# Reading the moving operand of the dense matmuls backwards, and writing PSUM backwards with it

## The chip, the cores and the metric

The kernel runs on one core of a Trainium2 chip. The metric is the device time of the whole kernel in microseconds (us), the median of several executions; lower is better. TensorE (PE in the rows) multiplies a stationary operand of up to 128 by 128 elements, loaded by a weight load (PEld), with a moving operand that is streamed through it column by column; the result goes to PSUM, eight banks of 512 float32 columns on each of 128 partitions. The other engines are VectorE (DVE), ScalarE (ACT), GpSimd (POOL) and SyncE (SP, which here issues the weight transfers).

## The reference, cut to what matters

One inference step of a two-layer decoder trunk for 256 prompt tokens and 8 sample tokens: a diagonal state-space layer, then an attention layer with compressed, selected and window branches. Nearly all of its arithmetic is dense products with float32 weights:

```python
D_MODEL, SEQ, DEC_BATCH, D_FF, PLE_DIM = 2048, 256, 8, 5632, 256

def swiglu(h, wg, wu, wd):
    return (jax.nn.silu(h @ wg) * (h @ wu)) @ wd

def compress_rows(rows, w1, b1, w2):        # paged K and V rows of 8 sequences of 2048
    ...
    w1p = w1.reshape(CMP_PARTS, CMP_STRIDE, HEAD_DIM, CMP_HIDDEN)
    h = b1
    for j in range(CMP_PARTS):
        h = h + jnp.einsum('bnsgd,sdh->bngh', units[:, j:j + n_cmp], w1p[j])
    return jax.nn.gelu(h) @ w2

# per layer: mixer, then x + swiglu(...), then
#   x = x + gate * (p[i] @ w['ple_w_proj'][i])   with gate from a 2048 x 2048 product
# between the layers: kv = rmsnorm(h) @ kv_w;  in the mixers: g @ w_glu, hn @ w_q, o @ w_o
```

## The kernel before

**Layout.** All activations stand transposed: channels on the partitions, the T = 264 tokens (256 prompt, 8 sample) as columns. A weight tile of 128 by 128 is the stationary operand and a [128, 264] slice of the activations the moving one.

**Precision.** A float32 product is made from three matmuls of the reduced type fp32r. A weight unit of 1024 columns is copied from `w_raw` to `w_head` by ScalarE (`split_head`, L377, which rounds), and VectorE takes the rest, `w_rest` = `w_raw` - `w_head` (`split_rest`, L381). The activations are split in the same way (`act_head` and `act_rest`, `hid_head` and `hid_rest`, `ple_head` and `ple_rest`). The product is then head by head, head by rest and rest by head, all three added into the same PSUM columns (L396, L397, L398).

**Dense groups.** `group_matmuls` goes through the units of a group. In each unit there are UK = 2 slices of the contraction, and for each slice four output tiles in four neighbouring PSUM banks, three matmuls each: 24 matmuls a unit. `phase_pe` calls it for the phases gate/up, down, per-layer embedding, kv, q and o; the glu phase (L1617, L1624) calls it with heads and rests in exchanged buffers (`act_rest` holds the heads there). Units come by SyncE transfers into a ring of RING = 4 slots: a transfer waits for `rest_done` of the unit that used the slot, ScalarE's copy for `raw_ready` and for `units_used` (TensorE's last matmul of the unit four back), VectorE's subtraction for the copy, TensorE for the subtraction.

**Page products.** The first stage has NITEM = 32 items (K or V, a sequence, a pair of heads). For each item, 32 transposes turn page rows (L1011), ScalarE and VectorE write them as `rows_head` and `rows_rest` [128, 16, 2, 130], and `taps_pe` multiplies them with the 32 taps: four parts of 8 taps, three matmuls each (L1032, L1033, L1034), 96 an item. The moving operand has 256 columns in two runs of 128 (two heads, 130 elements apart). For taps 0 to 15 (parts 0 and 1) each run begins at element 0 of its row, for taps 16 to 31 (parts 2 and 3) at element 1. The results go to columns 0 to 255 of bank 2 or 7. Between the parts TensorE turns the next item's pages and does the small matmuls of the state-space layer, whose scans and rotations run on VectorE, ScalarE and GpSimd beside it.

**Readers of the results.** GELU, the gates and the residual additions read the PSUM columns by their place in the bank. Full float32 matmuls (the small ones of the first stage, L1052 and L1055, the attention products L2108, L2172, L2198) and the transposes are not touched by the change; nor are the gate matmuls L1966 to L1968.

Of the kernel before, what the change touches and what calls it, by code (L numbers as in the profile page):

```python
# [19 lines left out]
P = 128  # L20
D, TP, TS, DEPTH = 2048, 256, 8, 2
T = TP + TS
# [86 lines left out]
def trunk_kernel(nc, io, out):  # L109
# [18 lines left out]
    WH = sb("w_head", [P, RING, SLOT], F32R)  # L128
    wl_at = sb.at
    WL = sb("w_rest", [P, RING, SLOT], F32R)  # L130
# [27 lines left out]
    ROWS_H, ROWS_L, rl_at = [None, None], [None, None], None  # L158
# [127 lines left out]
    PSUM = stack.enter_context(nc.psum_tensor("psum", [P, 8, 512], F32))  # L286
# [97 lines left out]
    def group_matmuls(pe, ph, i, c0, kunits, bank, heads, rests, ready):  # L384

        for ku in range(kunits):
            u = Unit(ph.base, ph.per, i, c0 + ku)
            pe.wait_ge(rest_done, u.n + 1)
            for kk in range(UK):
                k = UK * ku + kk  # L390
                if ready is not None:
                    ready(k)
                for n in range(4):
                    w = slice(kk * UN + n * P, kk * UN + (n + 1) * P)
                    o = PSUM[:, bank + n, 0:T]
                    nc.tensor.matmul(o, WH[:, u.slot, w], heads[:, k, :], start=k == 0, stop=False)  # L396
                    nc.tensor.matmul(o, WH[:, u.slot, w], rests[:, k, :], start=False, stop=False)  # L397
                    last = nc.tensor.matmul(o, WL[:, u.slot, w], heads[:, k, :], start=False,  # L398
                                            stop=k == UK * kunits - 1)
            last.then_inc(units_used, 1)  # L400

# [154 lines left out]
    def phase_pe(pe, name, heads, rests, norm=None, ready=None, heads_b=None, rests_b=None):  # L556
        ph = by_name[name]

        def first(k):
            if k == 8 and norm in NORMS:  # L560
                rms_pe(pe, norm)
            pe.wait_ge(xl_done, XLS[norm] + k + 1)

        def turn_early(k):
            if 2 <= k < 2 + EARLY:
                final_turn_pe(pe, k - 2)

        def body(i):
            at_first = norm is not None and isinstance(i, int) and i == 0
            pe.wait_ge(free_a, i + ph.groups)  # L570
            at_last = name == "ple1" and i == 3
            group_matmuls(pe, ph, i, 0, ph.ka, 0, heads, rests, first if at_first else turn_early if at_last else ready)
            pe.wait_ge(free_b, i + ph.groups)
            if at_last:
                pe.wait_ge(fin_used, EARLY)
            if at_first and norm in NORMS:
                pe.wait_ge(rt_done, NORMS[norm] + 1)
            group_matmuls(pe, ph, i, ph.ka, ph.kb, 4, heads_b or heads, rests_b or rests, None)

        steps_of(ph, pe, body)  # L580
# [342 lines left out]
    def mm_bank(k):  # L923
        return 2 if k % 2 == 0 else 7
# [89 lines left out]
    def taps_pe(pe, k, part):  # L1014
        if not 0 <= k < NITEM:
            return
        if part == 0:
            if k == 1:
                pe.wait_ge(rows_padded, 2)
            pe.wait_ge(cmp_rest, 8 * k + 8)  # L1020
            if k >= 2:
                pe.wait_ge(cmp_gelu, k - 1)
            if k - LEAD >= 0:
                pe.wait_ge(act_x, k - LEAD + 1)
        if k % (2 * NKV) == 0:
            pe.wait_ge(rest_done, RING * (k // (2 * NKV)) + part + 1)
        o = PSUM[:, mm_bank(k), 0:2 * P]
        for t in range(8 * part, 8 * part + 8):
            w = slice(t % 8 * P, (t % 8 + 1) * P)
            sh = t // 16  # L1030
            hi, lo = (r[k % 2][:, t % 16, :, sh:sh + P] for r in (ROWS_H, ROWS_L))
            nc.tensor.matmul(o, WH[:, part, w], hi, start=t == 0, stop=False)  # L1032
            nc.tensor.matmul(o, WH[:, part, w], lo, start=False, stop=False)  # L1033
            last = nc.tensor.matmul(o, WL[:, part, w], hi, start=False, stop=t == TAPS - 1)  # L1034
        last.then_inc(cmp_part, 1)
# [84 lines left out]
    def stage1_pe(pe):  # L1120
        for k in range(NITEM):
            p = k - LEAD
            taps_pe(pe, k, 0)
            turn_pages_pe(pe, k + 1, 0, 2)
            taps_pe(pe, k, 1)
            if k == 0:
                square_sums_pe(pe)
            turn_pages_pe(pe, k + 1, 2, 4)
            if k == NITEM - 1:
                turn_embeds_pe(pe, 0, DEPTH)  # L1130
            taps_pe(pe, k, 2)
            turn_pages_pe(pe, k + 1, 4, 6)
            if k == NITEM - 1:
                turn_embeds_pe(pe, DEPTH, 2 * DEPTH)
                second_pe(pe, k - 1)
            if p >= 1 and p % 2 == 1:
                turn_bc_pe(pe, p // 2 + 1)
            taps_pe(pe, k, 3)
            turn_pages_pe(pe, k + 1, 6, 8)
            if p == -1:  # L1140
                turn_bc_pe(pe, 0)
            inputs_pe(pe, p + 1)
            if k < NITEM - 1:
                second_pe(pe, k - 1)
            carried_pe(pe, p + 1, 1, pe_xs)
            outputs_pe(pe, p)
# [445 lines left out]
    def glu_pe(pe):  # L1592
# [21 lines left out]
        for i in range(ph.steps):  # L1614
            if i:
                pe.wait_ge(free_a, i)
            group_matmuls(pe, ph, i, 0, ph.ka, 0, XL, XH, first if i == 0 else states if i == 1 else None)  # L1617
            if i:
                pe.wait_ge(free_b, i)
            else:  # L1620
                pe.wait_ge(y_sum, KC)
            if i == 1:
                pe.wait_ge(fs_used, FS_JOBS)
            group_matmuls(pe, ph, i, ph.ka, ph.kb, 4, XL, XH, None)  # L1624
# [1345 lines left out]
```

## Time and profile before

| | |
|---|---|
| Median of 3 runs | 3335.01 us (3333.84 to 3336.41) |
| Span of the profiled execution | 3330.0 us |
| What lies around the span (median less span) | 5.0 us |
| TensorE busy | 3249.2 us, 98% |
| Weight loads busy | 3104.4 us, 93% |
| VectorE, ScalarE, GpSimd busy | 2034.1, 1466.8, 538.1 us |
| Matmuls | 27,900 |
[...]

A matmul's duration in the rows runs from its start to the end of its last column in PSUM, and the next one starts long before that end. So what a matmul costs in a dense stretch is read from the distance of one start to the next, or from the number of matmuls that a full stretch holds, and not from its own duration.

### The profile page before, as it was taken

What the parts mean: (1) busy time and instruction counts of PE and PEld (TensorE: products, weight loads), DVE (VectorE), ACT (ScalarE), POOL (GpSimd) and SP (SyncE); (2) the same over time, 40 slices, a digit from 0 to 9 for tenths busy, and PEclk for the clock granted to TensorE, in tenths of its full rate; (3) what the DMA queues carried; (4) which work ended last, traced back from release to release, by engine and by line L of the source; (5) the groups of instructions that cost most, each with busy time, mean ns of one, the idle gap of its engine ahead of it and who ended that gap; (6) DMA issues with size and microseconds to landing.
All of it is one profiled execution on the core that took longest, in us unless ns stands there. A gap on an engine that the chain in (4) does not pass through costs nothing.

```text
span 3330.0 us, 69559 instructions
## 1 busy us (share of the span) xinstructions
PE 3249.2 (98%) x27900; PEld 3104.4 (93%) x27900; DVE 2034.1 (61%) x2265; ACT 1466.8 (44%) x1943; POOL 538.1 (16%) x477
## 2 busy tenths in 40 slices
PE   7999999999999999999999999999999999999998
PEld 6888899989999999999999997865999999999998
DVE  7999888865654544555566555455665554455566
ACT  4555555543543433434445432344453433334444
POOL 5666566620000000001000005100000000000000
PEclk9999999999999999999999999999999999999999
DMA  6444544545556555565556658889565655565553
GB/s 179 140 137 138 161 148 142 160 138 179 169 170 189 179 181 179 177 183 177 184 176 188 181 199 274 288 282 298 184 185 176 184 182 178 176 183 182 179 172 132
DMA packets 384394, 608.45 MB, mean 183 GB/s; under 512 B 52537, under 2 KB 144986, under 8 KB 383882
## 3 DMA queue, kind: packets, MB, share of 16 engines
q1 hardware_dynamic: 360954, 555.84, 53.4%
q10 hardware_dynamic: 20176, 44.08, 4.0%
q0 software_dynamic: 3024, 5.22, 0.5%
q8 instruction: 164, 2.69, 0.3%
q14 instruction: 76, 0.62, 0.1%
HBM read 594.83 MB, written 26.94 MB: 187 GB/s over the span
## 4 chain that ended last, share of the span: by engine, by line
PE 75%; DVE 10%; issue 5%; POOL 5%; ACT 2%; SPq 1%; DMA 1%; POOLq 0%; DVEq 0%; ACTq 0%
PE psum L396 22%; PE psum L398 22%; PE psum L397 22%; DVE rows_rest L1332 2%; PE psum L2300 2%; DVE turned L1391 2%; PE psum L2310 1%; POOL prod_pool L1538 1%; PE psum L2348 1%; DVE state_ri L1399 1%; DVE w_rest L381 1%; POOL sines L1487 1%; PE psum L2172 1%; PE psum L2198 1%; POOL b_pad L1527 1%
## 5 line engine op out<-in xcount | busy, mean ns | idle before, releaser
L381 DVE TENSOR_TENSOR w_rest<-w_raw,w_head 128x1024 fp32r<-128x1024 f32 x776 | 974.1, 1267 | 960.9 <-ACT w_head L377 960.1
L377 ACT ACTIVATE w_head<-w_raw 128x1024 fp32r<-128x1024 f32 x776 | 812.3, 1056 | 1048.7 <-PE psum L398 1024.4
L396 PE MATMUL psum<-act_head,w_head 128*128 128x264 f32 x4224 | 1206.9, 286 | 4.9 <-DVE act_rest L2731 4.9
L398 PE MATMUL psum<-act_head,w_rest 128*128 128x264 f32 x4224 | 1202.5, 285 | 0.0
L397 PE MATMUL psum<-act_rest,w_head 128*128 128x264 f32 x4224 | 1200.8, 284 | 0.0
L396 PEld LDWEIGHTS psum<-act_head,w_head 128*128 128x128 f32 x4224 | 797.6, 189 | 5.7 <-issue 5.2
L397 PEld LDWEIGHTS psum<-act_rest,w_head 128*128 128x128 f32 x4224 | 799.6, 189 | 0.2
L398 PEld LDWEIGHTS psum<-act_head,w_rest 128*128 128x128 f32 x4224 | 798.0, 189 | 0.0
L396 PE MATMUL psum<-hid_head,w_head 128*128 128x264 f32 x1408 | 401.0, 285 | 0.0
L398 PE MATMUL psum<-hid_head,w_rest 128*128 128x264 f32 x1408 | 400.6, 285 | 0.0
L397 PE MATMUL psum<-hid_rest,w_head 128*128 128x264 f32 x1408 | 399.9, 284 | 0.0
L1725 POOL TENSOR_TENSOR hid_rest<-prod_val,hid_head 128x1056 f32 x22 | 54.3, 2470 | 1760.7 <-ACT hid_head L1692 1760.7
L1032 PE MATMUL psum<-rows_head,w_head 128*128 128x256 f32 x1024 | 303.6, 297 | 1.8 <-DVE rows_rest L1332 1.4
L1034 PE MATMUL psum<-rows_head,w_rest 128*128 128x256 f32 x1024 | 292.4, 286 | 0.0
L1033 PE MATMUL psum<-rows_rest,w_head 128*128 128x256 f32 x1024 | 291.8, 285 | 0.0
L397 PEld LDWEIGHTS psum<-hid_rest,w_head 128*128 128x128 f32 x1408 | 266.1, 189 | 0.0
L398 PEld LDWEIGHTS psum<-hid_head,w_rest 128*128 128x128 f32 x1408 | 265.6, 189 | 0.0
L396 PEld LDWEIGHTS psum<-hid_head,w_head 128*128 128x128 f32 x1408 | 265.5, 189 | 0.0
L1169 ACT ACTIVATE rows_head<-psum 128x512 fp32r<-128x512 f32 x256 | 140.5, 596 | 213.3 <-PE psum L1011 213.3
L1032 PEld LDWEIGHTS psum<-rows_head,w_head 128*128 128x128 f32 x1024 | 196.5, 192 | 14.7 <-issue 14.7
L1033 PEld LDWEIGHTS psum<-rows_rest,w_head 128*128 128x128 f32 x1024 | 197.0, 192 | 0.0
L1034 PEld LDWEIGHTS psum<-rows_head,w_rest 128*128 128x128 f32 x1024 | 196.4, 192 | 0.0
(420 smaller groups left out, 4126.3 us busy)
## 6 DMA issues: line engine op xcount, KB each, us to landing
w_raw<-in_ffn_w_gate SPq DMA_DIRECT2D x176, 512.0 KB, 4.2
w_raw<-in_ffn_w_up SPq DMA_DIRECT2D x176, 512.0 KB, 4.3
w_raw<-in_ffn_w_down SPq DMA_DIRECT2D x176, 512.0 KB, 3.6
w_raw<-in_cache_cmp_k SPq DMA_DIRECT2D x256, 128.0 KB, 2.5
w_raw<-in_cache_cmp_v SPq DMA_DIRECT2D x256, 128.0 KB, 2.6
w_raw<-in_ssm_w_glu SPq DMA_DIRECT2D x64, 512.0 KB, 3.8
w_raw<-in_ple_w_gate SPq DMA_DIRECT2D x64, 512.0 KB, 4.4
tiles<-in_cache_slc_v SPq DMA_DIRECT2D x128, 256.0 KB
```

The lines of the kernel that those rows point to most:

```text
L377: nc.scalar.activation(WH[:, u.slot, :], RAW[:, u.slot, :], ACT.Copy).then_inc(head_done, 1)
L381: nc.vector.tensor_tensor(WL[:, u.slot, :], RAW[:, u.slot, :], WH[:, u.slot, :].bitcast(F32), ALU.subtract).then_inc(rest_done, 1)
L396: nc.tensor.matmul(o, WH[:, u.slot, w], heads[:, k, :], start=k == 0, stop=False)
L397: nc.tensor.matmul(o, WH[:, u.slot, w], rests[:, k, :], start=False, stop=False)
L398: last = nc.tensor.matmul(o, WL[:, u.slot, w], heads[:, k, :], start=False, stop=k == UK * kunits - 1)
L1032: nc.tensor.matmul(o, WH[:, part, w], hi, start=t == 0, stop=False)
L1033: nc.tensor.matmul(o, WH[:, part, w], lo, start=False, stop=False)
L1034: last = nc.tensor.matmul(o, WL[:, part, w], hi, start=False, stop=t == TAPS - 1)
L1169: nc.scalar.activation(head_rows(k, m // 2, m % 2), page_rows(n), ACT.Copy).then_inc(cmp_head, 1)
L1332: nc.vector.tensor_tensor(rest_rows(k, m // 2, m % 2), page_rows(n), head_rows(k, m // 2, m % 2).bitcast(F32), ALU.subtract).then_inc(cmp_ ...
L1391: last = nc.vector.tensor_tensor_scan(GB[:, t, h, :], m, GB[:, t, h, :], 0.0, ALU.mult, ALU.add)
L2300: last = nc.tensor.transpose(PSUM[:, 2 * (u % 2) + e, g * P:(g + 1) * P], TILE[:, tile_slot(WK + u), at:at + DH], IDENT[:, :])
```

## The change

In `group_matmuls` and in `taps_pe` the moving operand is given with a negative step, so that its last column is read first, and the PSUM columns are given with a negative step too, so that the first result goes to the last column. Column j of the moving operand still ends in column j of the bank. In the page products both dimensions of the moving operand are turned round, the two heads and the 128 columns. The stationary operand, the number and order of the matmuls and every wait and signal stay as they are.

```diff
-                    o = PSUM[:, bank + n, 0:T]
-                    nc.tensor.matmul(o, WH[:, u.slot, w], heads[:, k, :], start=k == 0, stop=False)
-                    nc.tensor.matmul(o, WH[:, u.slot, w], rests[:, k, :], start=False, stop=False)
-                    last = nc.tensor.matmul(o, WL[:, u.slot, w], heads[:, k, :], start=False,
+                head, rest = heads[:, k, ::-1], rests[:, k, ::-1]
+                    o = PSUM[:, bank + n, T - 1::-1]
+                    nc.tensor.matmul(o, WH[:, u.slot, w], head, start=k == 0, stop=False)
+                    nc.tensor.matmul(o, WH[:, u.slot, w], rest, start=False, stop=False)
+                    last = nc.tensor.matmul(o, WL[:, u.slot, w], head, start=False,
                                             stop=k == UK * kunits - 1)
...
-        o = PSUM[:, mm_bank(k), 0:2 * P]
+        o = PSUM[:, mm_bank(k), 2 * P - 1::-1]
...
-            hi, lo = (r[k % 2][:, t % 16, :, sh:sh + P] for r in (ROWS_H, ROWS_L))
+            hi, lo = (r[k % 2][:, t % 16, :, sh:sh + P][:, ::-1, ::-1] for r in (ROWS_H, ROWS_L))
```

## Rows read from the trace of the kernel before

**Rows 1.** The page: busy time, its share of the span, instructions of each engine.

```profile
PE 3249.2 (98%) x27900; PEld 3104.4 (93%) x27900; DVE 2034.1 (61%) x2265; ACT 1466.8 (44%) x1943; POOL 538.1 (16%) x477
```

**Rows 2.** The page: shares of the chain that ended last, by engine and line.

```profile
PE 75%; DVE 10%; issue 5%; POOL 5%; ACT 2%; SPq 1%; DMA 1%; POOLq 0%; DVEq 0%; ACTq 0%
PE psum L396 22%; PE psum L398 22%; PE psum L397 22%; DVE rows_rest L1332 2%; PE psum L2300 2%; DVE turned L1391 2%; PE psum L2310 1%; POOL prod_pool L1538 1%; PE psum L2348 1%; DVE state_ri L1399 1%; DVE w_rest L381 1%; POOL sines L1487 1%; PE psum L2172 1%; PE psum L2198 1%; POOL b_pad L1527 1%
```

**Rows 3.** Windows of the first stage and of the rest: busy time, instructions, clock.

```profile
core 0: us, PE busy (x) PEld busy (x) DVE busy (x) ACT busy (x) POOL busy (x), PEclk, DMA share, GB/s
32.00:685.00 653.00, 630.03 (x5008) 581.47 (x5008) 566.57 (x709) 361.73 (x580) 393.34 (x356) 0.99 0.47 142
685.00:3320.00 2635.00, 2597.32 (x22786) 2507.43 (x22784) 1447.71 (x1511) 1088.62 (x1335) 127.83 (x93) 0.99 0.61 192
```

**Rows 4.** Windows of 50 us inside dense phases, the same columns.

```profile
1450.00:1500.00 50.00, 50.00 (x413) 50.00 (x412) 26.10 (x21) 19.74 (x19) 2.47 (x1) 1.00 0.60 181
2900.00:2950.00 50.00, 50.00 (x413) 50.00 (x412) 27.24 (x22) 19.19 (x19) 2.47 (x1) 1.00 0.59 179
```

**Rows 5.** TensorE's groups by line and shape: busy us, mean ns, idle before.

```profile
L396 PE MATMUL psum<-act_head,w_head 128*128 128x264 f32 x4224 | 1206.9, 286 | 4.9 <-DVE act_rest L2731 4.9
L396 PE MATMUL psum<-hid_head,w_head 128*128 128x264 f32 x1408 | 401.0, 285 | 0.0
L1032 PE MATMUL psum<-rows_head,w_head 128*128 128x256 f32 x1024 | 303.6, 297 | 1.8 <-DVE rows_rest L1332 1.4 <-ACT state_ri L1181 0.4
L396 PE MATMUL psum<-act_rest,w_head 128*128 128x264 f32 x512 | 147.5, 288 | 1.4 <-DVE w_rest L381 1.4
L396 PE MATMUL psum<-ple_head,w_head 128*128 128x264 f32 x64 | 18.2, 284 | 0.0
```

**Rows 6.** TensorE's timeline in the glu phase, where the granted clock is 0.50.

```profile
711.65 0.42 PE L396 MATMUL psum<-act_rest,w_head 128*128 128x264 f32 x1
711.87 0.42 PE L397 MATMUL psum<-act_head,w_head 128*128 128x264 f32 x1
...
714.73 0.42 PE L398 MATMUL psum<-act_rest,w_rest 128*128 128x264 f32 x1
```

**Rows 7.** The window that holds most of these matmuls.

```profile
708.30:714.90 6.60, 5.98 (x26) 4.63 (x27) 3.67 (x5) 1.82 (x3) 1.17 (x1) 0.50 0.73 205
```

**Rows 8.** TensorE's timeline in one item: parts 1 and 2 of the taps.

```profile
331.84 0.28 PE L1033 MATMUL psum<-rows_rest,w_head 128*128 128x256 f32 x1
...
334.49 0.28 PE L1034 MATMUL psum<-rows_head,w_rest 128*128 128x256 f32 x1
...
335.60 0.28 PE L1033 MATMUL psum<-rows_rest,w_head 128*128 128x256 f32 x1
...
338.24 0.29 PE L1034 MATMUL psum<-rows_head,w_rest 128*128 128x256 f32 x1
```

**Rows 9.** Timeline of the attention part: float32 matmuls, several merged in one row.

```profile
2254.34 1.13 PE L2198 MATMUL psum<-probs_t_p,v_rows 128*128 128x512 f32 x2
2261.11 1.06 PE L2172 MATMUL psum<-k_cmp_p,q_t 128*128 128x15 f32 x8
2270.42 1.98 PE L2198 MATMUL psum<-probs_t_p,v_rows 128*128 128x512 f32 x4
```

**Rows 10.** Timeline of L2108, whose moving operand steps by 16 elements.

```profile
2129.44 1.80 PE L2108 MATMUL psum<-kv_t,taps_p 128*128 128x60 f32 x14
```

**Rows 11.** Waits of the other engines, total us, times, longest.

```profile
ACT w_head L377 <- PE psum L398: 1024.4, 593, 5.0
DVE w_rest L381 <- ACT w_head L377: 960.1, 589, 3.4
```

## The prediction

> **What bounds the kernel now.** I read the page first. TensorE is busy 98% of the span and no other engine over 61% [rows 1], and the chain that ended last lies on TensorE for 75%, 66% of it on the three lines of the dense groups [rows 2]. A busy share says little for pipelined matmuls, so I went on to windows. In 50 us of a dense phase TensorE starts 413 matmuls without a gap: 50 / 413 = 121.1 ns a matmul of 264 columns [rows 4]. After the first stage TensorE is idle 2635 - 2597.3 = 38 us in all, in the first stage 653 - 630.0 = 23 us [rows 3]. VectorE and ScalarE wait for TensorE's last matmul of a unit or for each other (1024 and 960 us in all), so they have room [rows 11]. The reader is to see that every nanosecond added to or taken from a dense matmul's distance to the next goes into the time, nearly undiminished.
>
> How many are touched: each of the lines L396 to L398 has 4224 + 1408 + 512 + 64 = 6208 matmuls (the group with `act_rest,w_head` is the glu phase), 18,624 in all; the taps have 3 x 1024 = 3072 [rows 5]. The taps' distance is (334.49 - 331.84) / 22 = 120.5 ns in part 1 and (338.24 - 335.60) / 22 = 120.0 ns in part 2 [rows 8]; I take 120.3. So the touched matmuls hold 18,624 x 0.1211 + 3072 x 0.1203 = 2255 + 370 = 2625 us of the 3330 us. One nanosecond on each is 21.7 us, and 0.2% of the time, 6.7 us (about what a measurement of this kernel can tell from no change), is 0.31 ns on each.
>
> **What sets 121 ns.** [...] Matmuls of only 15 columns with a full stationary tile start about (1.06 - 0.28) / 7 = 111 ns apart [rows 9] (0.28 us for the last one's own duration), so the stationary side alone allows some 112 ns and no less.
>
> **The change, part by part.**
>
> 1. Instructions, waits, transfers: none added, removed or moved. Slices with a negative step are worked out when the program is built. 0 us.
>
> 2. Reading the moving operand backwards. No row has a backward read, so its cost is bounded. Two rows are near. In parts 2 and 3 of the taps each run starts one element later than in parts 0 and 1, and the distance is 120.0 against 120.5 ns [rows 8]: where a run begins against any grouping of elements costs nothing. L2108 reads its moving columns 16 elements apart, 60 of them per matmul, and 14 such matmuls take 1.80 us together, at most 129 ns each [rows 10]. They are full float32, which goes at (1.98 - 1.13) / 2 / 512 = 0.83 ns a column [rows 9], so 60 columns want 50 ns and the rest of the 129 hides up to 2.1 ns a column. That row therefore only says that even a far step costs no more than 2.1 ns a column. The bounds: 0 below, 2.1 ns a column above; backward by one element is much nearer to the unit step of the tap rows than to 16 elements, so I take 0.
>
> 3. Writing PSUM backwards. Every matmul in the trace writes upwards with unit step, so there is no row at all for another order. [...]
>
> The sum is 3330.0 + 0 for the span and 5.0 us around it: 3335 us, which is the median of the runs shown.
>
> [...]
>
> **The rivals.**
>
> [...]
> [...]
>
> [...]
>
> [...]
>
> *Each column on its own, far worse (slower).* With 2.1 ns a column, 264 columns take 0.57 us: 18,624 x 0.45 + 3072 x 0.43 = 9.7 ms more. This is only the bound of [rows 10]; nothing speaks for it.
>
> That the change does nothing to the hardware's work is the forecast itself.
>
> [...]
>
> **How the numbers follow.** Forecast, no change: 0.50. Two clocks a column: 0.30, since nothing in the trace tests the write order. Small cost per matmul: 0.12. Far worse: 0.03. Faster: 0.05. The predicted time is that of the likeliest, 3335 us; its own range is 3328 to 3342 us. The range that should hold the time 8 times in 10 has to take in the rival of 0.30, since without it only 0.62 is left: from 3325 to 5475 us, which holds 0.92, and no point between gives 0.8. Chances: faster by over 0.2% 0.05, within 0.2% 0.50, slower by over 0.2% 0.12 + 0.30 + 0.03 = 0.45.
>
> **What the changed profile would show.** If I am right, windows of 50 us in a dense phase again hold 412 to 414 matmuls, the taps stay at 120 ns, and TensorE's idle time stays. [...] If only the read or only the write is at fault, the profile cannot tell which; that takes a kernel that turns one alone. [...]

## The result, and the profile after

| | before | after |
|---|---|---|
| Median | 3335.32 us (4 runs) | 3314.62 us (3314.22 to 3317.57, 4 runs) |
| Ratio | | 0.9937, 95% interval 0.9923 to 0.9951 |
| Span of the profiled execution | 3330.0 us | 3313.1 us |

The kernel became 0.6% faster, some 21 us, where no change was forecast; 3314.62 us lies below the range as well, which began at 3325 us. The page of the changed kernel, as [rows 1] of before:

```profile
PE 3236.4 (98%) x27900; PEld 3091.0 (93%) x27900; DVE 2028.7 (61%) x2265; ACT 1467.0 (44%) x1943; POOL 536.5 (16%) x477
```

The same instructions, and TensorE busy for 12.8 us less. Windows of the changed kernel, as [rows 3] and [rows 4]: from and to, length, busy us and instructions of PE, PEld, DVE, ACT, POOL, clock, DMA share, GB/s.

```profile
32.00:685.00 653.00, 630.44 (x5014) 581.31 (x5013) 567.07 (x712) 364.12 (x583) 390.37 (x356) 0.99 0.47 142
685.00:3320.00 2635.00, 2585.74 (x22810) 2495.66 (x22808) 1448.41 (x1522) 1093.47 (x1344) 129.83 (x93) 0.99 0.61 193
1450.00:1500.00 50.00, 50.00 (x416) 50.00 (x415) 26.76 (x21) 19.74 (x19) 2.46 (x1) 1.00 0.60 179
2900.00:2950.00 50.00, 50.00 (x416) 50.00 (x415) 25.77 (x20) 20.09 (x20) 2.46 (x1) 1.00 0.63 189
```

In 50 us of a dense phase there are 416 matmuls and not 413: 120.2 ns each in place of 121.1. The first stage is as before. The waits answer to [rows 11]; ScalarE's and VectorE's waits shrink together by 25 us, as TensorE is done with each unit sooner:

```profile
ACT w_head L377 <- PE psum L399: 1010.1, 588, 4.8
DVE w_rest L381 <- ACT w_head L377: 949.0, 590, 3.4
```

Over all dense matmuls of the two traces (start to next start, gaps over 150 ns left out) the mean distance fell from 121.73 to 120.84 ns; times some 18,530 such distances this is 16.5 us of the 16.9 us by which the span shrank. The taps stayed at 120.4 and 120.5 ns.

**Where in the dense groups.** The distances are not scattered; they repeat with a period of four units, eight rows k of the activations. Two units in a row of the phase gu10, in the kernel before: first and last start of the second, and of the third unit of a group.

```profile
989.53 0.29 PE L396 MATMUL psum<-act_head,w_head 128*128 128x264 f32 x1
...
992.32 0.28 PE L398 MATMUL psum<-act_head,w_rest 128*128 128x264 f32 x1
992.43 0.29 PE L396 MATMUL psum<-act_head,w_head 128*128 128x264 f32 x1
...
995.26 0.28 PE L398 MATMUL psum<-act_head,w_rest 128*128 128x264 f32 x1
```

Each has 23 distances: 2.79 / 23 = 121.3 ns in the second unit, 2.83 / 23 = 123.0 ns in the third. The same two units of the changed kernel:

```profile
988.90 0.28 PE L397 MATMUL psum<-act_head,w_head 128*128 128x264 f32 x1
...
991.73 0.29 PE L399 MATMUL psum<-act_head,w_rest 128*128 128x264 f32 x1
991.85 0.28 PE L397 MATMUL psum<-act_head,w_head 128*128 128x264 f32 x1
...
994.62 0.28 PE L399 MATMUL psum<-act_head,w_rest 128*128 128x264 f32 x1
```

Now the second unit is the slow one, 2.83 / 23 = 123.0 ns, and the third goes at 2.77 / 23 = 120.4 ns. All units together, mean distance in ns by the unit's place modulo 4 in its group, worked out from all starts of the traces:

```
                    unit 1   unit 2   unit 3   unit 4
before, gu10        121.74   121.04   122.92   121.29
before, dn10        122.89   121.29   121.70   121.04
after,  gu10        120.11   123.02   120.14   120.07
after,  dn10        120.13   120.08   120.08   123.04
```

Backward there is a floor of 120.1 ns in three units of four, and one at 123.0. Forward no unit reaches the floor. A unit is the mean of two rows k. Row by row, in the gate/up phases of both traces, the spread is wider (ns):

```
k modulo 8      0      1      2      3      4      5      6      7
before        121.8  121.5  120.9  121.2  123.8  122.1  122.2  120.4
after         120.1  120.1  123.8  122.3  120.2  120.1  120.1  120.1
```

The place in the group sets the figure, and not the slot of the ring: in dn20, whose groups have ten units, the second group of a pair uses the slots shifted by two, and each place has the same distance in both groups to within 0.05 ns. The pattern is tied to addresses: a row of 264 float32 is 1056 bytes, four times 256 and 32 over, so row k begins at 128 + 32k modulo 256 in `act_head` and `act_rest`, and at 32k in `hid_head` and `hid_rest`, by the places in the kernel's layout. From gate/up to down that is a shift by 128 bytes, two units, and the patterns are shifted by just two units. Every weight slice of 128 columns begins at 128 modulo 256.

### The profile page after: what moved, and what is told of

It reads as the page before. It is cut to its first block, busy times and chain, and to the rows that moved or that the text cites. A ratio compares the mean times of both kernels' runs of the same rounds, so it can differ in the third digit from the quotient of the medians.

```text
span 3313.1 us, 69559 instructions
## 1 busy us (share of the span) xinstructions
PE 3236.4 (98%) x27900; PEld 3091.0 (93%) x27900; DVE 2028.7 (61%) x2265; ACT 1467.0 (44%) x1943; POOL 536.5 (16%) x477
## 4 chain that ended last, share of the span: by engine, by line
PE 76%; DVE 10%; POOL 5%; issue 5%; ACT 2%; DMA 1%; SPq 0%; POOLq 0%; DVEq 0%; ACTq 0%
PE psum L397 22%; PE psum L399 22%; PE psum L398 22%; DVE rows_rest L1333 2%; PE psum L2301 2%; DVE turned L1392 1%; PE psum L2311 1%; POOL prod_pool L1539 1%; PE psum L2349 1%; PE psum L2173 1%; PE psum L2199 1%; DVE state_ri L1400 1%; POOL sines L1488 1%; PE psum L1012 1%; POOL b_pad L1528 1%
## 5 line engine op out<-in xcount | busy, mean ns | idle before, releaser
L377 ACT ACTIVATE w_head<-w_raw 128x1024 fp32r<-128x1024 f32 x776 | 812.1, 1056 | 1035.0 <-PE psum L399 1010.1
```

The costliest lines, as they stand in the source:

```text
L377: nc.scalar.activation(WH[:, u.slot, :], RAW[:, u.slot, :], ACT.Copy).then_inc(head_done, 1)
```

## The experiments

Theories at the start: R, the gain comes from reading backward; W, from writing PSUM backward.

**e1_dense_only** turns round only the dense groups; **e2_taps_only** only the page products.

```diff
 # e1: against the changed kernel
-        o = PSUM[:, mm_bank(k), 2 * P - 1::-1]
+        o = PSUM[:, mm_bank(k), 0:2 * P]
-            hi, lo = (r[k % 2][:, t % 16, :, sh:sh + P][:, ::-1, ::-1] for r in (ROWS_H, ROWS_L))
+            hi, lo = (r[k % 2][:, t % 16, :, sh:sh + P] for r in (ROWS_H, ROWS_L))
 # e2: against the kernel before, the same lines the other way round
```

> Only the dense groups are turned round (reads and PSUM writes), the page products are as before. Theory R (the moving reads clash with another reader or writer of SBUF and meet it less often when they run backward) and theory W (the PSUM writes do) both put the whole gain here, since the dense matmuls went from 121.7 to 120.8 ns from start to start and the taps stayed at 120.4: about 3315 us, ratio 0.993 to 0.995, dense distance 120.8 ns. A theory that the gain came with the first stage would have 3335 us.

> Only the page products are turned round. By both theories nothing is left: 3335 us within 0.2%, dense distance 121.7 ns, taps 120.4 to 120.5 ns. If the first stage has a part in the gain, it shows as several us here.

Measured: e1 3318.23 us, ratio 0.9957 (0.9943 to 0.9972), mean dense distance 120.84 ns, as after. e2 3334.30 us, ratio 1.0005 (0.9996 to 1.0014), dense and tap distances as before. The page products have no measurable part in it. The median of e1 is somewhat above the forecast of 3315 and its ratio above 0.993 to 0.995; its interval overlaps that of the changed kernel.

**e3_read_only** and **e4_write_only** split the two halves of the change, in the dense groups.

```diff
 # e3: reads backward, writes forward
-                    o = PSUM[:, bank + n, T - 1::-1]
+                    o = PSUM[:, bank + n, 0:T]
 # e4: against the kernel before: reads forward, writes backward
-                    o = PSUM[:, bank + n, 0:T]
+                    o = PSUM[:, bank + n, T - 1::-1]
```

> In the dense groups the moving operand is read backward and PSUM is written forward, so that the tokens of each product come out mirrored (part of the computation is changed; its amount is not). Theory R: dense distance 120.8 ns with one in four unit positions at 123 ns, and 3315 us. Theory W: 121.7 ns, 3335 us.

> In the dense groups the moving operand is read forward and PSUM is written backward, so that the tokens of each product come out mirrored (part of the computation is changed; its amount is not). Theory R: dense distance 121.7 ns with the pattern of the kernel before, 3335 us. Theory W: 120.8 ns, 3315 us.

Measured: e3 3316.24 us, ratio 0.9954 (0.9937 to 0.9971); e4 3335.50 us, ratio 1.0003 (0.9993 to 1.0013). Windows of e3 and then of e4:

```profile
1450.00:1500.00 50.00, 50.00 (x416) 50.00 (x415) 28.06 (x22) 18.68 (x18) 2.46 (x1) 1.00 0.61 183
```

```profile
1450.00:1500.00 50.00, 50.00 (x413) 50.00 (x412) 25.99 (x21) 19.78 (x20) 2.47 (x1) 1.00 0.59 179
```

The unit means are those of after in e3 (120.1, 123.0, 120.1, 120.1 in gu10) and those of before in e4 (121.7, 121.0, 122.9, 121.3). Theory W falls: a backward write to PSUM costs nothing and gives nothing. Theory R stands. What remained was what the read meets.

**e5_weights_moved** and **e6_small_split** tell apart the other party of the clash.

```diff
 # e5
+    sb.at += 64
     wh_at = sb.at
 # e6
-        nc.scalar.activation(WH[:, u.slot, :], RAW[:, u.slot, :], ACT.Copy).then_inc(head_done, 1)
+        nc.scalar.activation(WH[:, u.slot, 0:u.cols], RAW[:, u.slot, 0:u.cols], ACT.Copy).then_inc(head_done, 1)
 # and likewise in split_rest; u.cols is 8 from the fifth unit of glu to the first of q, else 1024
 # both: dense groups only, with
+                step = 1 if ph.name in ("gu10", "dn10") else -1
```

> The two weight buffers that TensorE reads (and all that lies behind them, the hidden activations too) stand 64 bytes higher; the activations of the gate/up phases keep their place. The dense groups read backward, save the phases gu10 and dn10, which read forward. Before, the excess over 120 ns follows k modulo 8, that is the address of the activation row modulo 256 bytes. Theory C (clash of the moving reads with the stationary reads, set by their address difference): backward, the slow unit of four in gate/up moves from the second to the third, and in the down phases stays the fourth; forward, the dearest unit (122.9 ns) moves from the third to the fourth in gu10, and stays the first in dn10. Theory A (the activation row's own address, for instance where it meets a 256-byte border): the slow unit of gate/up stays the second, that of the down phases moves from the fourth to the third; forward, gu10 keeps the third, dn10 moves from the first to the fourth. Means stay 120.8 and 121.7 ns by both.

> In the units of glu to q, ScalarE and VectorE split only the first 8 of 1024 columns of a unit (the rest of the weights is stale; that part of the computation is left out), so their reads and writes of the weight buffers are gone. gu10 and dn10 read forward, all others backward. Theory C (TensorE's two reads clash with each other): distances as with full splits, forward 121.7 ns, backward 120.1 in three of four units and 123.0 in the fourth. Theory O (the other engines' accesses clash with the moving reads): all near 120.0 ns, about 0.8 to 1.7 ns less.

Measured, mean distances in ns:

```
                          unit 1   unit 2   unit 3   unit 4
e5 backward, gu11         120.12   120.13   123.02   120.15
e5 backward, dn11         120.12   120.10   120.08   123.04
e5 forward,  gu10         121.33   121.70   121.04   122.92
e5 forward,  dn10         122.89   121.30   121.70   121.04
e6 backward, gu20         120.09   123.04   120.12   120.08
e6 forward,  gu10         121.65   121.05   122.92   121.29
```

In e5 gate/up, whose activations did not move, all is shifted by one unit, and the down phases, where both operands moved by 64 bytes, stay as they were: what theory C asks for, to within 0.05 ns, and theory A falls. Second and third unit of gu11 in e5:

```profile
2522.26 0.28 PE L399 MATMUL psum<-act_head,w_head 128*128 128x264 f32 x1
...
2525.02 0.28 PE L401 MATMUL psum<-act_head,w_rest 128*128 128x264 f32 x1
2525.14 0.28 PE L399 MATMUL psum<-act_head,w_head 128*128 128x264 f32 x1
...
2527.97 0.29 PE L401 MATMUL psum<-act_head,w_rest 128*128 128x264 f32 x1
```

2.76 / 23 = 120.0 ns and 2.83 / 23 = 123.0 ns. In e6 the splitting engines have next to nothing to do with the weight buffers, and the distances are the same; theory O falls. The window (backward, phase gu20) has VectorE and ScalarE at 8.4 and 6.0 us of 50, and again 416 matmuls:

```profile
1320.00:1370.00 50.00, 50.00 (x416) 50.00 (x416) 8.41 (x20) 6.02 (x19) 2.45 (x1) 1.00 0.62 179
```

So the delay depends on the moving row's address less the stationary slice's address, modulo 256 bytes, and on the direction. By units, each the mean of two differences: backward 123.0 ns at 64 and 96 and 120.1 elsewhere; forward 121.7 at 0 and 32, 121.0 at 64 and 96, 122.9 at 128 and 160, 121.3 at 192 and 224. By single rows the dearest are 64 backward and 128 forward, both at 123.8, and forward 224 is near the floor, at 120.4. (e5 took 3320.82 and e6 3301.95 us, a single execution each; e6 leaves work out.)

**e7_mixed** takes the cheaper direction for each k.

```diff
-                head, rest = heads[:, k, ::-1], rests[:, k, ::-1]
+                step = 1 if (k + (4 if heads is HH else 0)) % 8 in (2, 3) else -1
+                head, rest = heads[:, k, ::step], rests[:, k, ::step]
 # and o forward where step is 1
```

> Dense groups read backward, save the two k of each eight where backward costs 123.0 ns and forward 121.0 ns; those read and write forward. Page products as before. Theories C and A: mean distance (3 x 120.1 + 121.0) / 4 = 120.3 ns, so 0.5 ns x 18,600 = 9 us below the changed kernel, about 3306 us, ratio 0.991 to 0.993. If a change of direction from one row to the next costs by itself, 3310 us or more.

Measured: 3319.48 us, ratio 0.9950 (0.9937 to 0.9964), as e1. The 3306 us of theories C and A did not come; the time is on the side of the other branch, 3310 us or more. The units read forward among backward ones stand at 123.4 ns, not at 121.0, while the others are at 120.0 to 120.1. First and last starts of the two forward rows in such a unit of gu10:

```profile
987.41 0.28 PE L398 MATMUL psum<-act_head,w_head 128*128 128x264 f32 x1
...
988.73 0.28 PE L400 MATMUL psum<-act_head,w_rest 128*128 128x264 f32 x1
988.86 0.29 PE L398 MATMUL psum<-act_head,w_head 128*128 128x264 f32 x1
...
990.24 0.29 PE L400 MATMUL psum<-act_head,w_rest 128*128 128x264 f32 x1
```

The first row goes at 1.32 / 11 = 120.0 ns, the second at 1.38 / 11 = 125.5 ns; over all gate/up phases it is 120.8 and 126.0, where forward throughout these rows have 120.9 and 121.2. So the price is not paid at the turn itself but all along the second row. Why is not shown. The 121.0 ns belong to a kernel that reads forward throughout; a table of such distances can't be put together piece by piece.

**e8_narrow** asks what the floor of 120 ns is.

```diff
 # all but the first matmul of a group stream columns 127 to 0 alone
+                half = slice(127, None, -1)
+                    nc.tensor.matmul(o[:, T - 128:], WH[:, u.slot, w], rests[:, k, half], start=False, stop=False)
 # likewise for the two others
```

> Each dense matmul but the three kinds' first of a group streams only 128 of the 264 columns, backward (the products of the other tokens are left out). If the 120 ns are set by the stationary side, the distance stays 120 ns and the excess of the slow unit shrinks; if they are the 264 columns (110 ns) and a fixed 10 ns, it falls to some 112 ns (the distance of the 15-column matmuls) or below.

Measured, a single execution: 4988.51 us, half as long again for half the columns. In the first microseconds of glu, at full clock, the distance is (701.01 - 700.68) / 3 = 110 ns here and 112 ns in the median:

```profile
700.68 0.27 PE L399 MATMUL psum<-act_head,w_head 128*128 128x128 f32 x1
700.79 0.28 PE L400 MATMUL psum<-act_rest,w_rest 128*128 128x128 f32 x1
700.90 0.28 PE L398 MATMUL psum<-act_rest,w_head 128*128 128x128 f32 x1
701.01 0.28 PE L399 MATMUL psum<-act_head,w_head 128*128 128x128 f32 x1
```

That is the second branch of the expectation, whose 110 ns for 264 columns can be had as an estimate from [rows 6]: half of the 220 ns at a granted clock of 0.50. Then the granted clock falls to 0.50, and stays there for most of the run (mean 0.604):

```profile
980.00:1470.00 490.00, 490.00 (x2296) 489.79 (x2295) 154.14 (x122) 118.55 (x117) 12.18 (x5) 0.50 0.34 102
```

TensorE is busy without a gap in these 490 us, and yet at a granted clock of 0.50: 490 / 2296 = 213.4 ns a matmul. The clock had last fallen at 838 us. Before that TensorE had held the full clock for 32 us with the same narrow matmuls, 287 without a gap, until it stopped for 1.47 us to wait for VectorE:

```profile
803.00:834.80 31.80, 31.80 (x287) 31.80 (x286) 17.35 (x14) 13.29 (x14) 0.00 (x0) 1.00 0.63 184
836.61 0.33 PE L398 MATMUL psum<-act_rest,w_head 128*128 128x128 f32 x1 [1.47 <-DVE w_rest L381]
850.00:2930.00 2080.00, 2080.00 (x9738) 2079.38 (x9739) 650.07 (x562) 503.14 (x516) 30.23 (x13) 0.50 0.34 103
```

From 838 us on it is at 0.50, and 2080 us without a gap did not bring the clock back. After an earlier stop in glu, of 4.3 us, 75 us without a gap went by at 0.50:

```profile
715.00:790.00 75.00, 75.00 (x353) 74.71 (x353) 25.18 (x22) 19.53 (x19) 0.00 (x0) 0.50 0.38 110
```

The kernel before stops at the same place in glu, for 3.9 us, and falls to 0.50 too [rows 7], but its matmuls of 264 columns are at 1.00 again from 715 us on:

```profile
715.00:720.00 5.00, 5.00 (x43) 5.00 (x43) 2.45 (x2) 1.06 (x1) 0.00 (x0) 1.00 0.50 145
```

So with 128 columns the distance is 112 ns at a granted clock of 1.00 and 213.4 ns at 0.50. At the rate of [rows 6], 220 / 264 = 0.83 ns a column at 0.50, 128 columns would take 107 ns there, and half of that, 53 ns, at 1.00 (estimates), and with 15 columns the distance was 111 ns too [rows 9]. So it is not the number of columns that sets these distances, and I put them down to the stationary side. The floor of 120 ns with 264 columns is 8 ns more.

**e12_narrow_one** narrows only one of the three.

```diff
-                    nc.tensor.matmul(o, WH[:, u.slot, w], rest, start=False, stop=False)
+                    nc.tensor.matmul(o[:, T - 128:], WH[:, u.slot, w], rests[:, k, 127::-1], start=False, stop=False)
```

> Dense groups backward; of the three matmuls of each product only the second (head weights by activation rests) streams 128 of the 264 columns, so that the clock may stay up (the rest of that term is left out). If 264 columns running beside a stationary load cost the 8 ns between the 112 ns of 128 columns and the 120 ns, the distance from the second to the third falls from 120 to about 112 ns and the two others stay at 120 ns, the mean at 117.5 ns, 3255 to 3265 us at a clock near 1. If 120 ns are a fixed price of a stationary load after a full one, all three stay at 120 ns.

Measured, a single execution: 3281.22 us, clock 0.989, 424 matmuls in 50 us. One product takes 1451.22 - 1450.86 = 0.36 us:

```profile
1450.86 0.29 PE L397 MATMUL psum<-act_head,w_head 128*128 128x264 f32 x1
1450.98 0.23 PE L398 MATMUL psum<-act_rest,w_head 128*128 128x128 f32 x1
1451.04 0.34 PE L399 MATMUL psum<-act_head,w_rest 128*128 128x264 f32 x1
1451.22 0.29 PE L397 MATMUL psum<-act_head,w_head 128*128 128x264 f32 x1
```

The mean, 50 / 424 = 117.9 ns, is close to the 117.5 of the first branch, but neither branch has the distances: the third starts early, 60 ns after the narrow one, and the next product some 175 ns later. Nor is the time within 3255 to 3265 us. Narrowing one of three gives back about 2 ns a matmul, and narrowing all three 8. The number of columns streamed beside a load has a part in the floor; how it adds up stays open.

**e9_slots_back** uses the address rule. Slots 0 and 2 of `w_head` and `w_rest` stay at 128 modulo 256, slots 1 and 3 go to 192, so that no row of gate/up or down stands 64 or 96 bytes from its weights. Three small tiles of the attention part (`soft_small`, `gates_s`, `b_gate`) move into the gap of 192 bytes, and the two that lay over the second half of `w_rest` begin behind it.

```diff
-    WH = sb("w_head", [P, RING, SLOT], F32R)
+    WHE = sb("w_head_e", [P, 2, SLOT], F32R)
+    sb.at += 64
+    WHO = sb("w_head_o", [P, 2, SLOT], F32R)
...
-    WL = sb("w_rest", [P, RING, SLOT], F32R)
+    WLO = sb("w_rest_o", [P, 2, SLOT], F32R)
+    gap_at = sb.at
+    sb.at += 192
+    WLE = sb("w_rest_e", [P, 2, SLOT], F32R)
```

> The changed kernel with the weight slots laid out anew: slots 0 and 2 of each buffer stay at address 128 modulo 256, slots 1 and 3 stand at 192, by a gap of 64 bytes in one buffer and of 192 in the other (into which three small tiles move). Theory C, with the slow address difference (row start less weight start) of 64 and 96 modulo 256: no unit of gate/up, down, glu, kv, q and o has that difference any more, all stand at 120.1 ns, only half of the per-layer embedding keeps slow ones. Mean from 120.84 to 120.15 ns, 0.7 ns x 18,600 = 13 us less than the changed kernel, about 3302 us, ratio 0.989 to 0.991. If the slow unit has another cause, some unit of four stays at 123 ns and the time near 3315 us.

> The changed kernel as it is, beside the others on the same chip. All theories: ratio 0.994, dense distance 120.84 ns, 17 us below the kernel before.

> The kernel before (everything read and written forward) with the same new layout of the weight slots. Theory C, with the forward distances of the kernel before by address difference (0 and 32: 121.7; 64 and 96: 121.0; 128 and 160: 122.9; 192 and 224: 121.3 ns): in gate/up the four units have 121.7, 121.7, 122.9, 122.9, in the down phases 122.9, 122.9, 121.7, 121.7; mean 122.3 ns, about 0.6 ns x 18,600 = 11 us slower than the kernel before. If the order of neighbouring rows matters as much as the difference, the figures are others. If only the direction matters, all stays at 121.7 ns.

Measured: e9 3304.82 us, ratio 0.9909 (0.9894 to 0.9924); e10, the changed kernel beside it, 3316.30 us, ratio 0.9938 (0.9924 to 0.9951). e9 beats both kernels. Its second and third unit of a group in gu10 go at (987.74 - 984.98) / 23 = 120.0 and (990.63 - 987.87) / 23 = 120.0 ns:

```profile
984.98 0.28 PE L413 MATMUL psum<-act_head,w_head_o 128*128 128x264 f32 x1
...
987.74 0.29 PE L415 MATMUL psum<-act_head,w_rest_o 128*128 128x264 f32 x1
987.87 0.29 PE L413 MATMUL psum<-act_head,w_head_e 128*128 128x264 f32 x1
...
990.63 0.29 PE L415 MATMUL psum<-act_head,w_rest_e 128*128 128x264 f32 x1
```

and its window holds 419 matmuls:

```profile
1450.00:1500.00 50.00, 50.00 (x419) 50.00 (x418) 27.43 (x21) 21.64 (x21) 4.92 (x2) 1.00 0.56 168
```

The mean over all dense matmuls is 120.29 ns, 0.55 ns under after, where 0.7 was expected: the second unit has 120.4, and the per-layer embedding keeps 120.2 to 121.6. What is left in gate/up sits in a single matmul of each unit. In all four units the first 23 distances are at 120.1 ns; the last, from the unit's last start to the next unit's first, is 126.7 ns in the second unit and 123.3 in the third (119.1 and 120.0 in the two others). The weight load that runs beside the unit's last matmul is already that of the next slot (here in the second unit, `w_head_e` beside `w_rest_o`):

```profile
987.74 0.29 PE L415 MATMUL psum<-act_head,w_rest_o 128*128 128x264 f32 x1
987.75 0.19 PEld L413 LDWEIGHTS psum<-act_head,w_head_e 128*128 128x128 f32 x1
```

Against the next slot's address the last rows of these two units do stand at 96; the layout had avoided that only within a unit. So the address that counts is that of the weights loaded beside a matmul, not of the weights that it multiplies by: this is the closest view of the clash that the runs give.

e11, the same layout read forward, has (ns):

```
                     unit 1   unit 2   unit 3   unit 4
expected, gu10       121.7    121.7    122.9    122.9
measured, gu10       121.24   121.49   122.70   122.80
expected, dn10       122.9    122.9    121.7    121.7
measured, dn10       122.57   122.88   121.21   121.54
```

The order of cheap and dear units is as the address rule has it, each 0.0 to 0.5 ns lower; that the neighbouring rows act on it is likely after e7, but not shown. The mean is 122.03 ns (before 121.73), half of the rise to 122.3 that was expected; the single execution took 3334.07 us, so the 6 us of loss that the mean gives don't show in a single time.

## Why the prediction was wrong, point by point

**What bounds the kernel** held. One nanosecond on each dense matmul went nearly undiminished into the time: 0.89 ns gave 16.5 us in the trace, 21 us between the medians.

**The step that failed is part 2 of the change**, the backward read, which was put at exactly 0 between bounds of 0 and 2.1 ns a column. Its lower bound excluded a gain without a reason. It measured -0.89 ns a matmul of 264 columns (e3), 0.0 in the page products (e2). The two rows behind the 0 could not carry it. L2108 [rows 10] only bounds a cost from above. The tap rows [rows 8] compare two starts one element, 4 bytes, apart, in matmuls of 256 columns where the backward read does nothing either. From them the prediction took that where a run begins costs nothing; in the dense rows, whose starts step by 32 bytes, it costs up to 3.4 ns (120.4 to 123.8). What would have helped stood in the same trace, in rows that I did not read: unit by unit the dense distances differ by 1.9 ns, in a pattern of four units that follows the activations' addresses. A price that depends on the address of an operand is a sign that its reading order may matter too.

**Part 3**, the backward write at 0, was right (e4, ratio 1.0003), although no row of before tested the write order and the 0 was my guess. The rival of two clocks a column, which had 0.30 and stretched the range to 5475 us, did not come, and no run shows its price: 50 us of a dense phase hold 413 matmuls in e4 and 416 in the changed kernel. Nor does a run show the small cost per matmul, which had 0.12: one unit in four got dearer, from 121.0 to 123.0 ns in gu10, and the three others cheaper.

**The rival "faster"**, at 0.05, is what came, by 0.6%, and its chance rested on no row. Of the 121.1 - 112 = 9.1 ns between the distance of before [rows 4] and that of the stationary side alone [rows 9], 0.9 went. What vanished is what lay over 120.1 ns, in three units of four, while the fourth got dearer (121.0 to 123.0 ns in gu10). The backward PSUM writes have no part in it (e4, ratio 1.0003), nor have the other engines' accesses to the weight buffers (e6, distances as with full splits to within 0.1 ns); the address that counts beside that of the moving read is that of the weights being loaded (e5, e9). The taps did not gain (e2, 3334.30 us).

**What sets 121 ns.** The prediction had one row for it, the 111 ns of 15 columns [rows 9]. The runs show 112 ns with 128 columns (e8), which I put down to the stationary side; 120 ns with 256 or 264 columns streamed; and on top up to 3 ns by units, 3.7 by rows, which follow the difference between the addresses of moving row and weights modulo 256 bytes, and the direction (e5, e6, e9). Shifting the weights by 64 bytes moves a delay of 3 ns from one unit to the next (e5). That it is a clash between TensorE's own two reads is my reading of this.

**What stays open.** Why backward is slow at two address differences of eight (123.8 and 122.3 ns) and forward at all but one (120.9 to 123.8 ns): no run here shows it. Why a forward row among backward ones costs 126.0 ns (e7). Why the taps, with 256 columns in two runs, are at 120.4 ns in both directions. And what the 8 ns from 112 to 120 are made of (e12).

## What to carry to other kernels

Where TensorE is saturated, look at the distances from start to start unit by unit before costing a change to an operand's address, pitch or order: here a pattern that repeated with the row address was a delay that a layout avoided, 0.3% for 256 bytes of padding in the right places, on top of 0.6% for the direction (e9 against after, after against before). A bound of zero from below needs a reason of its own. Count with the weights that are being loaded, so with the next slot's at a unit's end (e9). And test a combination as a whole: distances measured in a steady stream did not hold when directions alternated (e7).

## What the runs showed of the hardware that was not expected

- A step of minus one cost nothing on the PSUM side of a matmul (e4: 3335.50 us, ratio 1.0003), and on the SBUF side it was cheaper than plus one (e3: 120.84 against 121.73 ns).
- A matmul's distance depends on where its moving row stands against the weights loaded beside it: read backward, at an address difference of 96 modulo 256, single matmuls stand at 126.7 and 123.3 ns among others at 120.1 (e9).
- Matmuls with 128 moving columns held the full clock for 32 us, but once it had fallen to 0.50 after a stop, 2080 us of them without a gap did not bring it back, and the kernel took 4988.51 us for less work (e8). With one of three matmuls narrowed the mean was 0.989 (e12). Cutting columns here gained at most 8 ns a matmul and cost half the clock.
- At a granted clock of 0.50, 264 columns stand at 220 ns [rows 6] and 128 columns at 213.4 ns (e8); at 1.00, 256 and 264 columns both stand near 120 ns (taps 120.4, dense floor 120.1) and 128 columns at 112 ns (e8).
